# Merging the two halves of the grouped-query mix: two ScalarE copies and a Pool addition, with the queues ordered anew

## The chip, the cores and the metric

One core of one Trainium2 chip. The metric is the device time of one execution in microseconds (us); the time before is the median of three runs. One more execution was taken with the hardware profiler; all rows of the trace are of that one. The engines are TensorE (PE; PEld is its weight load), VectorE (DVE), ScalarE (ACT), Pool (GpSimd) and SyncE (SP), whose queue issues the DMAs.

## What is computed

A one-layer encoder runs over a prompt of 1024 tokens and a sample of 512 tokens, all in float32 with a width of 1024. Cut to what matters here:

```python
h = rmsnorm(x, norm_mix_g)
dq, dk, dv, gq, gk, gv = split(h @ w_in)            # 512, 512, 512, 512, 128, 128 columns
d_out = diff_attention(dq, dk, dv, lam)             # 4 heads, values 128 wide
g_out = gqa_attention(gq, gk, gv)                   # 8 query heads of 64, 2 key/value heads
#   per head: softmax(q k^T * scale) @ v, v is 64 wide
x = x + concat(d_out, g_out) @ w_out
x = x + cross_attention(rmsnorm(x), rmsnorm(mem))
x = x + (silu(a) * b) @ w_down,  [a|b] = dwconv3(rmsnorm(x) @ w_up)
y = rmsnorm(x)
```

The change lies in `softmax(...) @ v` of the grouped-query heads.

## The kernel before

The kernel has two phases with a barrier of all engines between them. The trunk phase makes the input projection and both attentions; the rest phase does the output projection, cross attention and the feed-forward part. The diff touches only the trunk phase, which fills the first 875 us.

The trunk works through six units: four differential heads (units 0 to 3) and two groups of grouped-query heads (units 4 and 5). While one unit's attention runs, TensorE also makes the next unit's projections tile by tile (`proj`, then `nat`, `rope`, `qk_turn`, `qk_hi`, `qk_lo`, `v_split`). During unit 5 no projections are left. A unit's attention goes by pairs: a pair is one head with two query tiles of 128 rows, against 1024 keys (a long pair, prompt) or 512 keys (a short pair, sample). There are 24 differential and 48 grouped-query pairs, 24 in each of units 4 and 5, first the 16 long ones, then the 8 short ones.

The steps of a grouped-query pair are:

- `score` (TensorE, L882 and L883), once per query tile, into one of two PSUM slots `t_scores`
- `max` (VectorE, L1153), `exp` (ScalarE, L1017), `inverse` (VectorE, L1158), `scale` (Pool, L758) on the probabilities in SBUF
- `turn` (TensorE, L896): four transposes of 128x128 for each chunk of 256 keys, into one of two PSUM slots `t_turn`
- `hi` (ScalarE, L1026) and `lo` (VectorE, L1173): the transposed chunk split into a rounded high half and the remainder, each in one of two buffers. The next turn into the same PSUM slot waits for `lo`
- `mix` (TensorE, L917): the chunk's products with the values, summed into the accumulator `t_acc` over all chunks of the pair. The stationary operand holds the values' high half in 64 columns and their low half in the other 64, so rows 0 to 63 of `t_acc` have one part of the result and rows 64 to 127 the other, and both have to be added
- `out` (ScalarE, L1043): copies rows 64 to 127 of `t_acc` into `sq`, after the `merge` of the pair before
- `merge` (VectorE, L1192): adds rows 0 to 63 of `t_acc` and `sq` into `mixed`, after the store of two pairs ago, which read the same slot of `mixed`
- `store` (SyncE, L624): writes `mixed` to DRAM. The first `mix` of the next pair waits for the `merge`, since there is one accumulator

Float32 accuracy of the matmuls comes from such high and low halves, here as everywhere in the kernel.

The order of each engine's queue is not written by hand. `plan` puts each step with a due time, a duration and its predecessors, and `Plan.placed` walks through them: on each engine, the step whose wait goes least beyond that engine's `PATIENCE` comes first, and among those the one with the earliest rank. The rank is the due time moved by a number in `SHIFT`, one for each kind of step and stage (`dl`, `ds`, `gl`, `gs` are long and short pairs of differential and grouped-query units; `g` and `d` are the projections). The result is five fixed queues. The waits in the code stand for the data, so an order changes when a thing runs, not what it computes.

In the same phase Pool also splits the output weights (`out_split`, L681 and L684) during unit 5, and ScalarE and VectorE split the first two tiles of the next phase (`mix_hi` L1048, `mix_lo` L1197). At the end of the phase SyncE issues the last store, all engines meet at the barrier, and TensorE starts with L1981.

Of the kernel before, what the change touches and what calls it, by code (L numbers as in the profile page):

```python
# [33 lines left out]
ALU = mybir.AluOpType  # L34
# [3 lines left out]
P = 128  # L38
# [9 lines left out]
HD = 64  # L48
# [59 lines left out]
def unit_pairs():  # L108
# [4 lines left out]
    for u, (kind, _) in enumerate(UNITS):  # L113
        diff = kind == "diff"
        begin = now
        for seg, (t0, S) in enumerate(SEGS):
# [16 lines left out]

PATIENCE = {"PE": 0.03, "DVE": 0.23, "ACT": 0.36, "POOL": 0.23, "SP": 0.0}
SHIFT = {
    "dl": {"coef": -20.2, "combine": 6, "eps_r": 29.7, "exp": 3.9, "finish": 8.6, "hi": 7.7, "inverse": -50.1, "lo": 9, "max":
          19.8, "mix": 5.2, "out": 11.2, "score": 1.3, "spread": -12.7, "store": 5.4, "sub_mean": 2, "sub_rstd": 11, "sumsq":
          -72.3, "turn": -0.5},
    "ds": {"coef": -18.7, "combine": -16.4, "eps_r": -16.7, "exp": -3.3, "finish": -31.2, "hi": -6.7, "inverse": 43.7, "lo": 8.4,
          "max": -15.7, "mix": 5.1, "out": 7.2, "score": -5.6, "spread": -0.8, "store": 0.8, "sub_mean": 21.1, "sub_rstd": -38.7,  # L140
          "sumsq": -22.8, "turn": 1.8},
    "gl": {"exp": -5.7, "hi": -3.5, "inverse": -0.7, "lo": -21.9, "max": -3.2, "merge": -28.7, "mix": 1, "out": -2.2, "scale": 0.3,
          "score": -1.7, "store": 28.5, "turn": 0.4},
    "gs": {"exp": -4.8, "hi": -4, "inverse": -1.6, "lo": -1.4, "max": -4.5, "merge": -0.6, "mix": -36.7, "out": -2.9, "scale":
          -0.6, "score": -0.2, "store": -13.7, "turn": 2.5},
    "g": {"head_mean": -7.2, "head_norm": -8.8, "head_rstd": 16.7, "nat": -2.6, "proj": 0.1, "qk_hi": -42.5, "qk_lo": 15.5,
         "qk_turn": 0.2, "rope_add": 1.6, "rope": 8, "turn_round": -15.5, "v_split": 16.5},
    "d": {"nat": -42.3, "proj": -2.8, "qk_hi": 47.1, "qk_lo": 19.3, "qk_turn": 0.2, "rope": 5.3, "v_split": 9.7},
}
# [79 lines left out]
def plan(pairs, bounds):  # L229
# [115 lines left out]
    for p in pairs:  # L345
# [40 lines left out]
        whole = ("combine", (p, p.score + 3)) if p.diff else ("scale", (p, p.score + 1))  # L386
        merged = None if prev is None else ("out", (prev,)) if prev.diff else ("merge", (prev,))
        for c in range(p.chunks):
            b = first + space * c
            older = (p, c - 2) if c >= 2 else (prev, prev.chunks + c - 2) if prev else None  # L390
            put("PE", b, 0.46, "turn", (p, c), whole, ("turn", (p, c - 1)) if c else None)
            put("ACT", b + 0.6, 0.6, "hi", (p, c), ("turn", (p, c)), ("mix", older) if older else None)
            put("DVE", b + 1.25, 0.69, "lo", (p, c), ("hi", (p, c)))
            put("PE", b + space + 0.05, 0.72 if p.diff else 0.5, "mix", (p, c), ("lo", (p, c)), ("mix", (p, c - 1)) if c else merged,
                ("v_split", (tiles,)), ("nat", (NT - 1,)) if p.no == 0 else None)
# [10 lines left out]
        else:  # L406
            put("ACT", b, 0.38, "out", (p,), ("mix", (p, p.chunks - 1)), merged)
            put("DVE", b + 0.4, 0.42, "merge", (p,), ("out", (p,)))
            put("SP", b + 1.0, 0.07, "store", (p,), ("merge", (p,)))
# [15 lines left out]
def trunk_phase(nc, sems, a, key_scratch, value_scratch, split_x, mix_scratch, ident, half, wo_hi, wo_lo, wo_raw, h_hi, h_lo, h_raw):  # L425
# [13 lines left out]
    with ExitStack() as ctx:  # L439
# [118 lines left out]
        def stored_before(p):  # L558
            return mixed_stored[p.no % 2], 16 * (p.no // 2)
# [83 lines left out]
        def _(pool):  # L643
            nc.gpsimd.memset(ones[:, :], 1.0).then_inc(consts_made, 1)
            steps = 0
            for _, kind, what in order["POOL"]:
# [107 lines left out]
                elif kind == "scale":  # L754
                    p, n = what
                    pool.wait_ge(inv_done, n - 2 * n_diff + 1)
                    pr = prob[:, n % PSLOTS, 0:p.keys]
                    nc.gpsimd.tensor_scalar(pr, pr, inv[:, n % COLS:n % COLS + 1], 1.0, ALU.mult, ALU.mult).then_inc(scaled, 1)  # L758
                elif kind == "eps_r":
                    p, = what  # L760
# [19 lines left out]
        def _(pe):  # L780
# [7 lines left out]
            for _, kind, what in order["PE"]:  # L788
# [110 lines left out]
                elif kind == "mix":  # L899
# [3 lines left out]
                    if c == 0:  # L903
                        pe.wait_ge(v_split, p.unit * NT + (PT if p.seg == 0 else NT))
                        if p.no > n_diff:
                            pe.wait_ge(merged, p.no - n_diff)
                        elif p.no:
                            pe.wait_ge(copied, p.no)
                        else:
                            pe.wait_ge(nat_filled, NT)  # L910
# [24 lines left out]
        def _(act):  # L935
            for _, kind, what in order["ACT"]:
# [90 lines left out]
                elif kind == "out":  # L1027
# [10 lines left out]
                    else:  # L1038
                        if p.no > n_diff:
                            act.wait_ge(merged, p.no - n_diff)  # L1040
                        else:
                            act.wait_ge(spread_done, n_diff)
                        nc.scalar.copy(sq[0:HD, :], ps_o[HD:P, 0:2 * P]).then_inc(copied, 1)  # L1043
                elif kind == "mix_hi":
# [18 lines left out]
        def _(dve):  # L1063
            steps = 0
            for _, kind, what in order["DVE"]:
# [116 lines left out]
                elif kind == "finish":  # L1182
# [4 lines left out]
                                                   ps_t[:, slot, 0:2 * P], ALU.mult, ALU.mult).then_inc(finished, 1)  # L1187
                elif kind == "merge":
                    p, = what
                    dve.wait_ge(*stored_before(p))  # L1190
                    dve.wait_ge(copied, p.no + 1)
                    nc.vector.tensor_tensor(mixed[0:HD, p.no % 2, :], ps_o[0:HD, 0:2 * P], sq[0:HD, :], ALU.add).then_inc(merged, 1)  # L1192
                elif kind == "mix_lo":
# [1483 lines left out]
```

## Time and profile before

| | before |
|---|---|
| median of 3 runs | 2425.55 us (2425.24 to 2426.47) |
| the profiled execution | 2424.22 us |
| its span in the trace | 2422.4 us |
| TensorE busy | 2358.4 us (97%) |
| VectorE busy | 1695.5 us (70%) |
| ScalarE busy | 1017.0 us (42%) |
| Pool busy | 1393.4 us (58%) |
| mean granted TensorE clock | 0.994 |

The span is what the trace covers; 1.8 us of the profiled execution lie outside it. A row by line names the line of the kernel, the engine, the operation, what it writes and reads with their shapes, the count, the busy time with the mean of one, and how long the engine stood idle just before, with what it then waited for. In a row of a stretch each engine has its busy time with the number of instructions in brackets. TensorE's matmuls overlap in its pipeline, so its busy time is the time in which at least one is in flight.

### The profile page before, as it was taken

Reading aid. Unit: us, or ns where it says so; the run is one execution under the profiler, and the core shown is the slowest. Engines: PE = TensorE matmul, PEld = TensorE weight load, DVE = VectorE, ACT = ScalarE, POOL = GpSimd, SP = SyncE. Lnnn points to the kernel's source line nnn. Section 1 sums busy time; section 2 is a strip of 40 time slices with the busy share of each in tenths; the row PEclk is TensorE's granted clock in tenths of the full one; section 3 lists DMA queues with packets and bytes.
Section 4 is the critical chain, followed back from the end, with each engine's and each line's share of the span. In section 5 each row is a group of like instructions: output and inputs, shape, how many; then the busy total and the mean of one; then the engine's idle time right before and its main releaser. Section 6 shows DMA issues by size and latency. Waiting matters only on the chain.

```text
span 2422.4 us, 34257 instructions
## 1 busy us (share of the span) xinstructions
PE 2358.4 (97%) x12306; PEld 2021.4 (83%) x12306; DVE 1695.5 (70%) x2503; ACT 1017.0 (42%) x2048; POOL 1393.4 (58%) x1603
## 2 busy tenths in 40 slices
PE   7999999999999999999999999999989999999997
PEld 6999888888898878888888888888778888888886
DVE  7537777788989963243334388877688878887887
ACT  4436656555668851133332213211233333333334
POOL 5454645689877630052320277776677777777774
PEclk9999999999999999999999999999999999999999
DMA  8643444432212062131344322322321111111112
GB/s 298 247 174 136 157 144 159 153 129 98 94 61 85 13 195 104 59 116 61 120 144 137 140 95 96 105 95 88 131 98 55 53 53 53 53 53 52 53 53 92
DMA packets 102583, 260.40 MB, mean 107 GB/s; under 512 B 10128, under 2 KB 45328, under 8 KB 91920
## 3 DMA queue, kind: packets, MB, share of 16 engines
q1 hardware_dynamic: 101120, 257.82, 30.9%
q8 instruction: 100, 1.64, 0.3%
q14 instruction: 67, 0.55, 0.1%
q10 hardware_dynamic: 1296, 0.39, 0.1%
HBM read 209.95 MB, written 48.23 MB: 107 GB/s over the span
## 4 chain that ended last, share of the span: by engine, by line
PE 59%; DVE 2%; POOL 1%; issue 1%; ACT 1%; DMA 1%; SPq 0%; POOLq 0%; DVEq 0%; ACTq 0%
PE r_bank L2075 29%; PE r_bank L1981 11%; PE r_bank L1952 10%; PE r_bank L2014 5%; PE r_bank L2033 1%; PE r_bank L2062 1%; PE r_bank L1996 1%; DVE r_conv L2416 1%; PE r_bank L2045 0%; DMA r_rows_w<-in_w_up_units 0%; DVE r_x_p L2575 0%; ACT r_conv L2277 0%; POOL r_s_raw L1861 0%; DVE r_x_p L2564 0%; SPq L1727 0%
## 5 line engine op out<-in xcount | busy, mean ns | idle before, releaser
L843 PE MATMUL t_proj<-t_w_hi,t_hbuf 128*128 128x384 f32 x1056 | 312.7, 349 | 2.1 <-ACT t_nat L994 0.7
L2494 DVE TENSOR_TENSOR r_x_p<-r_bank,r_x_p 128x512 f32<-128x512 f32 x320 | 208.6, 683 | 50.9 <-PE r_bank L2075 50.1
L2416 DVE SCALAR_TENSOR_TENSOR r_conv<-r_rows,r_taps,r_conv 128x511 f32<-128x511 f32 (+1 forms) x132 | 181.8, 1377 | 54.3 <-ACT r_conv L2277 52.0
L1153 DVE TENSOR_REDUCE t_max_neg<-t_scores 128x1 f32<-128x1024 f32 (+1 forms) x192 | 197.0, 1038 | 23.4 <-PE t_scores L877 17.3
L1017 ACT ACTIVATE t_prob<-t_scores,t_max_neg 128x1024 f32<-128x1024 f32 (+1 forms) x192 | 187.3, 977 | 49.9 <-DVE t_max_neg L1153 45.7
L843 PEld LDWEIGHTS t_proj<-t_w_hi,t_hbuf 128*128 128x128 f32 x1056 | 195.7, 190 | 8.3 <-issue 6.8
L1026 ACT CAST t_pt_hi<-t_turn 128x512 fp32r<-128x512 f32 x240 | 140.1, 586 | 108.0 <-PE t_turn L896 82.3
L1173 DVE TENSOR_TENSOR t_pt_lo<-t_turn,t_pt_hi 128x512 fp32r<-128x512 f32 x240 | 163.5, 686 | 29.8 <-ACT t_pt_hi L1026 26.2
L843 PE MATMUL t_proj<-t_w_lo,t_hbuf 128*128 128x384 f32 x528 | 178.5, 338 | 0.0
L1762 POOL TENSOR_TENSOR r_stat<-r_stat,minus_half 128x1 f32<-128x1 f32 x24 | 14.1, 587 | 273.7 <-DVE r_stat L2379 273.7
L1817 POOL TENSOR_TENSOR r_w_lo<-r_stage,r_w_hi 128x1024 fp32r<-128x1024 f32 (+1 forms) x86 | 166.2, 1933 | 7.2
L2246 ACT CAST r_s_hi<-r_s_raw 128x512 fp32r<-128x512 f32 x88 | 54.6, 620 | 229.9 <-POOL r_s_raw L1868 87.0
L896 PE MATMUL t_turn<-ident,t_prob 128*128 128x128 f32 x960 | 142.5, 274 | 6.2 <-DVE t_pt_lo L1173 4.2
L917 PE MATMUL t_acc<-t_pt_hi,t_v_hi 128*128 128x256 f32 x480 | 138.8, 306 | 2.7 <-DVE t_mixed L1192 1.4
L1834 POOL TENSOR_TENSOR r_s_lo<-r_s_raw,r_s_hi 128x512 fp32r<-128x512 f32 x88 | 116.8, 1327 | 39.1 <-ACT r_s_hi L2246 39.1
L1814 POOL TENSOR_SCALAR r_w_hi<-r_stage 128x1024 fp32r<-128x1024 f32 (+1 forms) x86 | 84.4, 982 | 93.6 <-PE r_bank L2075 48.8
L2428 DVE TENSOR_TENSOR r_x_s<-r_bank,r_x_s 128x512 f32<-128x512 f32 x176 | 120.3, 688 | 24.8 <-PE r_bank L2075 23.0
L1952 PE MATMUL r_bank<-r_hs_hi,r_w_hi 128*128 128x512 f32 x352 | 137.1, 389 | 0.0
L1952 PE MATMUL r_bank<-r_hs_lo,r_w_hi 128*128 128x512 f32 x352 | 136.9, 389 | 0.0
L1952 PE MATMUL r_bank<-r_hs_hi,r_w_lo 128*128 128x512 f32 x352 | 136.9, 389 | 0.0
L896 PEld LDWEIGHTS t_turn<-ident,t_prob 128*128 128x128 f32 x960 | 111.8, 140 | 24.5 <-issue 11.8
L2075 PE MATMUL r_bank<-r_wd_lo,r_g_hi 128*128 128x512 f32 x336 | 130.7, 389 | 0.0
(299 smaller groups left out, 7282.3 us busy)
## 6 DMA issues: line engine op xcount, KB each, us to landing
t_hbuf<-split_x SPq DMA_DIRECT2D x60, 1024.0 KB, 4.8
r_stage<-in_w_up_units SPq DMA_DIRECT2D x44, 512.0 KB, 3.2
r_rows_w<-in_w_up_units SPq DMA_DIRECT2D x88, 256.0 KB, 2.9
split_x<-t_hbuf SPq DMA_DIRECT2D x12, 1024.0 KB, 5.2
r_stage<-in_w_down SPq DMA_DIRECT2D x22, 512.0 KB, 3.3
r_wd_raw<-in_w_down SPq DMA_DIRECT2D x42, 256.0 KB, 2.7
t_stage<-in_w_in_units SPq DMA_DIRECT2D x6, 1536.0 KB, 6.6
t_xkv_raw<-in_w_xkv_heads SPq DMA_DIRECT2D x16, 512.0 KB, 5.8
```

The costliest lines, as they stand in the source:

```text
L843: ins = nc.tensor.matmul(proj_bank(i), l, r[:, k, :], start=(k == 0 and j == 0), stop=(k == KT - 1 and j == 2))
L896: ins = nc.tensor.transpose(ps_t[:, slot, kk * 2 * P + qt * P:kk * 2 * P + (qt + 1) * P], prob[:, n % PSLOTS, keys], ident[:, :])
L1017: nc.scalar.activation(prob[:, n % PSLOTS, 0:p.keys], ps_s[:, n % 2, 0:p.keys], ACT.Exp, bias=max_neg[:, n % COLS:n % COLS + 1], accum_out ...
L1026: nc.scalar.copy(pt_hi[:, n % 2, :], ps_t[:, slot, :]).then_inc(pthi_done, 1)
L1153: nc.vector.tensor_reduce(max_neg[:, n % COLS:n % COLS + 1], ps_s[:, n % 2, 0:p.keys], AX.X, ALU.max, negate=True).then_inc(max_done, 1)
L1173: nc.vector.tensor_tensor(pt_lo[:, n % 2, :], ps_t[:, slot, :], f32(pt_hi[:, n % 2, :]), ALU.subtract).then_inc(ptlo_done, 1)
L1817: nc.gpsimd.tensor_tensor(lo, raw, f32(hi), ALU.subtract).then_inc(w_split[s], 1)
L1952: ins = nc.tensor.matmul(one_bank(s), l, r, start=(k == 0 and j == 0), stop=(k == KT - 1 and j == 2))
L1981: ins = nc.tensor.matmul(acc(t)[:, cols], l[:, k, :], r[:, cols], start=(k == 0 and j == 0), stop=(k == KT - 1 and j == 2))
L2075: ins = nc.tensor.matmul(out, l, r, start=(first and j == 0), stop=(last and j == 2), skip_group_check=onto)
L2416: return nc.vector.scalar_tensor_tensor(out, src, tap_of(j, s, i), out, ALU.mult, ALU.add)
L2494: nc.vector.tensor_tensor(x_p[:, t, cols], down_bank(n), x_p[:, t, cols], ALU.add).then_inc(p_add, 1)
```

## The change

`out` of a grouped-query pair now makes two ScalarE copies out of the accumulator: rows 0 to 63 into `mixed` and rows 64 to 127 into `sq`. `merge` moves to Pool and adds `sq` to `mixed` in place in SBUF. The wait for the store of two pairs ago moves with the first writer of `mixed` from VectorE's queue to ScalarE's. The first `mix` of a pair now waits for the copies (`copied`) and not for the merge. In the plan, `out` takes 0.8 in place of 0.38 and `merge` 0.55 on Pool in place of 0.42 on VectorE, with the new predecessors. All of `PATIENCE` but SyncE's and nearly all of `SHIFT` have new values, so that the queues of the whole trunk phase are placed anew.

```diff
-PATIENCE = {"PE": 0.03, "DVE": 0.23, "ACT": 0.36, "POOL": 0.23, "SP": 0.0}
+PATIENCE = {"PE": 0, "DVE": 0.47, "ACT": 0.38, "POOL": 0.72, "SP": 0.0}
 SHIFT = {
...
-    "gl": {"exp": -5.7, "hi": -3.5, "inverse": -0.7, "lo": -21.9, "max": -3.2, "merge": -28.7, "mix": 1, "out": -2.2, "scale": 0.3,
-          "score": -1.7, "store": 28.5, "turn": 0.4},
-    "gs": {"exp": -4.8, "hi": -4, "inverse": -1.6, "lo": -1.4, "max": -4.5, "merge": -0.6, "mix": -36.7, "out": -2.9, "scale":
-          -0.6, "score": -0.2, "store": -13.7, "turn": 2.5},
+    "gl": {"exp": 14.4, "hi": -3.9, "inverse": -2.3, "lo": -13.5, "max": -7.7, "merge": -22.4, "mix": 1.3, "out": -4, "scale":
+          -0.4, "score": -1.5, "store": 26.1, "turn": 0.4},
+    "gs": {"exp": 1.6, "hi": -9.5, "inverse": -1.5, "lo": -1.8, "max": -4, "merge": -44.3, "mix": -23.4, "out": -2.5, "scale": 18,
+          "score": 3.8, "store": -50.6, "turn": 1.1},
...
-            put("ACT", b, 0.38, "out", (p,), ("mix", (p, p.chunks - 1)), merged)
-            put("DVE", b + 0.4, 0.42, "merge", (p,), ("out", (p,)))
+            put("ACT", b, 0.8, "out", (p,), ("mix", (p, p.chunks - 1)), copied if prev.diff else ("merge", (prev,)),
+                ("store", (pairs[p.no - 2],)))
+            put("POOL", b + 0.9, 0.55, "merge", (p,), ("out", (p,)))
...
+                elif kind == "merge":
+                    p, = what
+                    pool.wait_ge(copied, p.no + 1)
+                    nc.gpsimd.tensor_tensor(mixed[0:HD, p.no % 2, :], mixed[0:HD, p.no % 2, :], sq[0:HD, :], ALU.add).then_inc(merged, 1)
...
-                        if p.no > n_diff:
-                            pe.wait_ge(merged, p.no - n_diff)
-                        elif p.no:
+                        if p.no:
                             pe.wait_ge(copied, p.no)
...
+                        act.wait_ge(*stored_before(p))
+                        nc.scalar.copy(mixed[0:HD, p.no % 2, :], ps_o[0:HD, 0:2 * P])
                         nc.scalar.copy(sq[0:HD, :], ps_o[HD:P, 0:2 * P]).then_inc(copied, 1)
...
-                elif kind == "merge":
-                    p, = what
-                    dve.wait_ge(*stored_before(p))
-                    dve.wait_ge(copied, p.no + 1)
-                    nc.vector.tensor_tensor(mixed[0:HD, p.no % 2, :], ps_o[0:HD, 0:2 * P], sq[0:HD, :], ALU.add).then_inc(merged, 1)
```

## Rows read from the trace of the kernel before

**Rows 1.** The page's busy times of the whole span.
```profile
PE 2358.4 (97%) x12306; PEld 2021.4 (83%) x12306; DVE 1695.5 (70%) x2503; ACT 1017.0 (42%) x2048; POOL 1393.4 (58%) x1603
```
**Rows 2.** Stretches (from:to, length): PE, PEld, DVE, ACT, POOL busy, clock, DMA.
```profile
160.00:480.00 320.00, 316.59 (x1965) 282.90 (x1964) 229.24 (x431) 188.20 (x503) 175.79 (x401) 1.00 0.44 155
480.00:597.00 117.00, 112.19 (x691) 97.70 (x690) 100.31 (x186) 67.04 (x154) 102.50 (x179) 1.00 0.34 120
597.00:750.00 153.00, 150.13 (x1018) 140.20 (x1018) 134.98 (x266) 108.59 (x237) 121.06 (x186) 1.00 0.19 65
750.00:830.00 80.00, 78.78 (x563) 71.78 (x562) 77.58 (x134) 71.47 (x132) 63.33 (x62) 1.00 0.22 66
830.00:873.00 43.00, 37.93 (x258) 31.00 (x256) 36.78 (x76) 34.33 (x77) 13.39 (x19) 1.00 0.17 42
...
600.00:620.00 20.00, 18.38 (x126) 16.97 (x126) 16.85 (x32) 12.69 (x27) 18.63 (x29) 1.00 0.26 88
```
**Rows 3.** Waits, 590 to 880: total us, times, longest.
```profile
POOL t_prob L758 <- DVE t_inv L1158: 49.9, 35, 3.9
PE t_turn L896 <- DVE t_pt_lo L1173: 4.2, 5, 1.3
...
PE t_acc L917 <- DVE t_mixed L1192: 1.4, 2, 1.0
PE t_scores L882 <- ACT t_prob L1017: 1.3, 3, 0.7
PE t_acc L917 <- DVE t_pt_lo L1173: 1.2, 2, 0.6
...
PE t_turn L896 <- POOL t_prob L758: 0.9, 1, 0.9
PE t_turn L932 <- DVE t_pt_lo L1173: 0.5, 1, 0.5
```
**Rows 4.** Groups by line on VectorE, 590 to 880.
```profile
L1173 DVE TENSOR_TENSOR t_pt_lo<-t_turn,t_pt_hi 128x512 fp32r<-128x512 f32 x159 | 108.3, 686 | 13.4 <-ACT t_pt_hi L1026 10.9
...
L1192 DVE TENSOR_TENSOR t_mixed<-t_acc,t_sq 64x256 f32<-64x256 f32 x48 | 19.6, 408 | 2.9 <-ACT t_sq L1043 2.0 <-DMA mix_scratch<-t_mixed 0.8
```
**Rows 5.** Groups by line on ScalarE, 750 to 830 (two rows) and 830 to 873.
```profile
L1026 ACT CAST t_pt_hi<-t_turn 128x512 fp32r<-128x512 f32 x55 | 32.3, 587 | 7.9 <-PE t_turn L896 3.7 <-PE t_acc L917 1.0
...
L1043 ACT COPY t_sq<-t_acc 64x256 f32<-64x256 f32 x14 | 5.2, 370 | 0.4
...
L1043 ACT COPY t_sq<-t_acc 64x256 f32<-64x256 f32 x12 | 4.4, 369 | 2.1 <-PE t_acc L917 1.7
```
**Rows 6.** In order of time, the phase's end: start us, length, engine, line.
```profile
870.11 0.37 ACT L1043 COPY t_sq<-t_acc 64x256 f32<-64x256 f32 x1
870.73 0.41 DVE L1192 TENSOR_TENSOR t_mixed<-t_acc,t_sq 64x256 f32<-64x256 f32 x1
871.28 0.36 PE L917 MATMUL t_acc<-t_pt_hi,t_v_hi 128*128 128x256 f32 x1 [0.95 <-DVE t_mixed L1192]
...
872.64 0.37 ACT L1043 COPY t_sq<-t_acc 64x256 f32<-64x256 f32 x1 [1.55 <-PE t_acc L917]
873.11 0.42 DVE L1192 TENSOR_TENSOR t_mixed<-t_acc,t_sq 64x256 f32<-64x256 f32 x1 [1.30 <-ACT t_sq L1043]
...
874.93 0.47 PE L1981 MATMUL r_bank<-wo_hi,h_hi 128*128 128x512 f32 x1 [2.33 <-PEq L439]
```
**Rows 7.** The tile t_mixed: idle before its instructions, and its DMAs' landing.
```profile
  DMA mix_scratch<-t_mixed: 0.8, 1
...
DMA to landing us min/median/max: 1.7/1.9/7.5
```
**Rows 8.** Single lines: nanoseconds min/median/max, first and last start.
```profile
L750 POOL TENSOR_TENSOR t_nat<-t_rot_a,t_rot_b x24: 726/736/764, 483.9 to 747.2; 128x256 f32<-128x256 f32 x24
...
L684 POOL TENSOR_TENSOR wo_lo<-wo_raw,wo_hi x16: 1273/1290/1305, 762.9 to 808.9; 128x512 fp32r<-128x512 f32 x16
...
L1116 DVE TENSOR_TENSOR t_rot_a<-t_nat x24: 472/493/1343, 474.8 to 737.2; 128x320 f32<-128x320 f32 x24
```

More of the change, by code:

```diff
@@ L131 @@
 RING = {"turn": "lo", "qk_turn": "qk_lo", "sumsq": "sub_mean", "spread": "finish", "total": "mean"}
-PATIENCE = {"PE": 0.03, "DVE": 0.23, "ACT": 0.36, "POOL": 0.23, "SP": 0.0}
+PATIENCE = {"PE": 0, "DVE": 0.47, "ACT": 0.38, "POOL": 0.72, "SP": 0.0}
 SHIFT = {
[L136 to L141, printed above, removed]
-    "gl": {"exp": -5.7, "hi": -3.5, "inverse": -0.7, "lo": -21.9, "max": -3.2, "merge": -28.7, "mix": 1, "out": -2.2, "scale": 0.3,
-          "score": -1.7, "store": 28.5, "turn": 0.4},
-    "gs": {"exp": -4.8, "hi": -4, "inverse": -1.6, "lo": -1.4, "max": -4.5, "merge": -0.6, "mix": -36.7, "out": -2.9, "scale":
-          -0.6, "score": -0.2, "store": -13.7, "turn": 2.5},
-    "g": {"head_mean": -7.2, "head_norm": -8.8, "head_rstd": 16.7, "nat": -2.6, "proj": 0.1, "qk_hi": -42.5, "qk_lo": 15.5,
-         "qk_turn": 0.2, "rope_add": 1.6, "rope": 8, "turn_round": -15.5, "v_split": 16.5},
-    "d": {"nat": -42.3, "proj": -2.8, "qk_hi": 47.1, "qk_lo": 19.3, "qk_turn": 0.2, "rope": 5.3, "v_split": 9.7},
@@ new lines @@
+    "dl": {"coef": -7.6, "combine": 21.4, "eps_r": 30, "exp": 5.8, "finish": 15.4, "hi": 10.3, "inverse": -62.4, "lo": 9.9, "max":
+          20.1, "mix": 5.1, "out": 23.7, "score": 1.4, "spread": 1.6, "store": 19.8, "sub_mean": 4.8, "sub_rstd": 22.6, "sumsq":
+          -61.9, "turn": -0.4},
+    "ds": {"coef": 2.9, "combine": -26.7, "eps_r": -30.8, "exp": -2, "finish": -52.6, "hi": -7.8, "inverse": 39.2, "lo": 15.8,
+          "max": -13, "mix": 8.3, "out": -0.2, "score": -8.4, "spread": 5.8, "store": 13.5, "sub_mean": 29, "sub_rstd": -39.7,
+          "sumsq": -50, "turn": 1.5},
@@ new lines @@
+    "gl": {"exp": 14.4, "hi": -3.9, "inverse": -2.3, "lo": -13.5, "max": -7.7, "merge": -22.4, "mix": 1.3, "out": -4, "scale":
+          -0.4, "score": -1.5, "store": 26.1, "turn": 0.4},
+    "gs": {"exp": 1.6, "hi": -9.5, "inverse": -1.5, "lo": -1.8, "max": -4, "merge": -44.3, "mix": -23.4, "out": -2.5, "scale": 18,
+          "score": 3.8, "store": -50.6, "turn": 1.1},
+    "g": {"head_mean": -2.1, "head_norm": 4, "head_rstd": 16.3, "nat": -3.7, "proj": 0.1, "qk_hi": -34.5, "qk_lo": 12.6,
+         "qk_turn": 0.4, "rope_add": -5.4, "rope": 16.2, "turn_round": -18, "v_split": 14.6},
@@ L149 @@
+    "d": {"nat": -27, "proj": -2.6, "qk_hi": 47.7, "qk_lo": 29.7, "rope": 8.4, "v_split": 9.2},
 }
@@ L386, in plan @@
         whole = ("combine", (p, p.score + 3)) if p.diff else ("scale", (p, p.score + 1))
-        merged = None if prev is None else ("out", (prev,)) if prev.diff else ("merge", (prev,))
+        copied = None if prev is None else ("out", (prev,))
         for c in range(p.chunks):
@@ L393, in plan @@
             put("DVE", b + 1.25, 0.69, "lo", (p, c), ("hi", (p, c)))
-            put("PE", b + space + 0.05, 0.72 if p.diff else 0.5, "mix", (p, c), ("lo", (p, c)), ("mix", (p, c - 1)) if c else merged,
+            put("PE", b + space + 0.05, 0.72 if p.diff else 0.5, "mix", (p, c), ("lo", (p, c)), ("mix", (p, c - 1)) if c else copied,
                 ("v_split", (tiles,)), ("nat", (NT - 1,)) if p.no == 0 else None)
```

## The prediction

> **What bounds the kernel now.** I read the busy table first. TensorE is busy 2358.4 us of 2422.4 [rows 1], so all that any edit outside TensorE's own work can give back is 64 us, and most of that is not where the change is. The second view is the table of stretches [rows 2]. It splits the trunk phase by what runs in it: 160 to 480 is the first three differential units, 480 to 597 the last of them beside the first grouped-query projections, 597 to 750 grouped-query unit 4 beside the projections of unit 5, 750 to 830 the long pairs of unit 5, 830 to 873 its short pairs. The reader is to take the stretch less its PE column: 3.4, 4.8, 2.9, 1.2 and 5.1 us, together 17.4 us of idle TensorE. The grouped-query part, where merges run, has 9.2 us of it. The other columns of the same rows tell which helper is closest to full: VectorE has 77.6 of 80 us in the long pairs of unit 5 (97%), ScalarE 71.5 (89%); in the short pairs they have 36.8 and 34.3 of 43; in unit 4 VectorE has 135.0, Pool 121.1 and ScalarE 108.6 of 153. TensorE sits at 98% beside a VectorE at 97%, so a full VectorE doesn't by itself mean a stalled TensorE.
>
> The third view is who TensorE waited for there [rows 3]. Waits for VectorE's low halves (L1173) are 4.2, 1.2 and 0.5 us, together 5.9. Waits for the merge (L1192) are 1.4 us in two places. ScalarE's exponential cost 1.3, Pool's scaling 0.9. The 2.3 us at L439 are the barrier between the two phases. Nothing behind the barrier is touched by the diff, and its order is made by another plan, so the whole argument is about these microseconds and about what the new order does with the 8.2 us ahead of 597.
>
> **What is taken away and what it gives.** 48 additions on VectorE of 408 ns, 19.6 us [rows 4]. They are not on the path by themselves: the two places where TensorE waited for one are worth 1.4 us. The accumulator t_acc is now free when ScalarE's second copy ends. Before, in the next to last pair, ScalarE's copy began at 870.11, the addition began at 870.73 and ended at 871.14, and TensorE went on at 871.28 [rows 6]: 1.03 us from copy to release. Two copies of 0.37 are 0.74, so 0.3 us is gained in each such place and all of the wait only if something else was early too. I take 0.8 us for the two (bounds 0.6 and 1.4).
>
> The larger part is the relief of VectorE's queue: 19.6 us of the 249.8 that it works from 597 to 876, where the low halves wait behind merges. It can give at most the 5.9 us of waits for low halves. I take 2.5, a little under half: VectorE was idle 10.9 us waiting for ScalarE's high half before low halves [rows 4], and that part of their lateness doesn't go when VectorE is emptier. Bounds 0 and 5.9.
>
> **What is added, ScalarE.** One more copy of 64x256 for each of 48 pairs at 369 to 370 ns [rows 5], 17.7 us. The same copy shows 14 times in the long pairs of unit 5 and 12 times in the short ones [rows 5]. In the long pairs ScalarE goes from 71.5 to 71.5 + 14 x 0.37 = 76.7 of 80 us (96%), while VectorE falls by 14 x 0.41 to 71.9: the two change places. In the short pairs it goes from 34.3 to 34.3 + 12 x 0.37 = 38.7 of 43 (90%). A copy out stands ahead of a high half or an exponential in ScalarE's queue, and each such high half comes 0.37 us later. It reaches TensorE where this already waits for low halves: four places in the short pairs, 4 x 0.37 = 1.5 us, which I take. Bounds: nothing, and 24 x 0.37 = 8.9 us if it happens at each pair of unit 5. The cover that hides the rest is TensorE's other queued work (the mix of the chunk before, the scores of the next pair); in unit 5 no projections are left to fill in.
>
> ScalarE now also waits for the store of two pairs ago. Behind it stand the high halves and exponentials of the next pair, and TensorE behind those. A store lands in 1.9 us at the median and 7.5 at most, and VectorE was held up by one once for 0.8 us [rows 7]. That one moves to ScalarE; I count it at nothing (bounds 0 and 0.8), since a pair takes over 3 us and the store is two pairs old.
>
> **What is added, Pool.** 48 additions of 64x256. The trace has none of that shape; the nearest are an addition with 256 columns at 736 ns and, above it, a subtraction with 512 columns at 1290 [rows 8]. From the 256-column row I take 0.74 us; the lower end is half of the first, 0.37, if 64 partitions cost half of 128, the upper 1.29. That is 35.5 us. In unit 4 Pool goes from 121.1 to 121.1 + 24 x 0.74 = 138.8 of 153 us (91%) and becomes the fullest of the three helpers there. A merge ahead of a scaling delays it by 0.74, and the transposes wait for the scaling. Pool stood idle 49.9 us before scalings, waiting for VectorE's reciprocal [rows 3], so nearly all merges fit in those holes; one that doesn't, in the crowded first 20 us of unit 4 [rows 2] or at a late pair, costs 0.7 us. Taken: +0.7. Bounds 0 and 24 x 0.74 = 17.8.
>
> The Trainium skill has a rule against moving this to Pool: "SBUF — State Buffer", section "SBUF: two separate sides", says that VectorE and GpSimd take turns by an exclusive lock on a shared port pair, which a VectorE instruction with two SBUF inputs and a GpSimd instruction that reads SBUF both want. The rows agree that such VectorE work stretches: the square at L1116 has a median of 493 ns and a maximum of 1343 [rows 8]. By the page the removed addition, with one input in PSUM, freed nothing of that lock and the new one takes it.
>
> **The end of the phase.** All engines meet at the barrier. Before, the last copy began at 872.64 and the last merge ended at 873.53, and TensorE's first matmul of the next phase came at 874.93 [rows 6]. The chain is now 0.37 + 0.37 + about 0.1 for the handover (872.64 + 0.37 to 873.11 shows it) + 0.74 on Pool = 1.58 instead of 0.89. Nothing hides it: +0.7 us (bounds 0.3 and 1.2).
>
> **The order placed anew.** Ranks and patience change for all kinds, the differential units too. Nothing in the trace shows the new order. It can give back no more than the 17.4 us of idle [rows 2], less what I counted above, and it can add as much. VectorE's place for low halves is the cause of most waits [rows 3], and it is what ranks decide; with 19.6 us less to place, the plan has more room than before. I take -2.0 us (bounds -9 and +7).
>
> **The sum.** -0.8 - 2.5 + 1.5 + 0 + 0.7 + 0.7 - 2.0 = -2.4 us. The profiled execution took 2424.2 us (span 2422.4 and 1.8 around it), so 2421.8; the median of the runs shown is 1.3 us above it, so 2423.1 us.
>
> **The rivals.** A measurement of this kernel can tell about 0.2%, 4.9 us, from no change: faster means under 2420.7, slower over 2430.4.
> *Most of the idle is given back.* If all 5.9 us of low-half waits and 1.4 us of merge waits go and the new order finds some 2 us more ahead of 597, less 0.7 at the barrier, the sum is -8.6 us: 2417. For it: VectorE is the fullest helper in each grouped-query stretch. Against it: ScalarE is put at 96% in its place, and much of the low halves' lateness comes from ScalarE.
> *ScalarE takes VectorE's place as what is late* (the slower side). In the long pairs of unit 5 it has 3 us of slack in 80 after the change. If its second copy delays a high half in each of the 24 pairs and TensorE has nothing else queued, 24 x 0.37 = 8.9 us, with 0.7 at the barrier and little given back: +8.5, 2434. It decides from the point where TensorE runs out of ready mixes, as it does already in the short pairs. Against it: from 750 to 830 ScalarE was idle 7.9 us ahead of high halves, of which the row names 4.7 as waits for TensorE [rows 5].
> *Pool is late in unit 4.* 91% full, with every scaling on the path to the transposes: half of 24 merges that each push a scaling by 0.74 are 8.9 us: 2433. For it: Pool was already 18.6 of 20 us busy from 600 to 620, where TensorE stood idle 1.6 us [rows 2], over half of what it lost in unit 4; a lock that stretches both sides would add to it. By the skill's page each clash could hold either engine for a whole instruction.
> *It does nothing that can be seen*: TensorE's work is the same and the waits only change their names: 2425.
>
> **How the numbers follow.** The forecast's case has 0.52; its own range is 2417 to 2429, and about a third of it (0.18) lies under 2420.7, so it gives 0.18 to faster and 0.34 to same. The idle given back has 0.18 (faster), nothing to be seen 0.06 (same), ScalarE late 0.14 and Pool late 0.10 (slower). Together faster 0.36, same 0.40, slower 0.24. The range leaves out the far part of the best and the worst cases: 2414.5 to 2433.5.
>
> **What the profile after would show.** Right: L1192 gone from VectorE, 96 copies of 0.37 us on ScalarE, waits of TensorE for L1173 down to about 3 us between 597 and 873, no wait for a merge, Pool's addition near 0.74 us, and 0.7 us more between the last copy and the first L1981. Wrong: waits of L896 or L917 for low halves that stand or grow, with VectorE idle before them for L1026 (ScalarE's rival); L896 waiting for L758 in several places (Pool's); or the idle from 160 to 597 moving by more than 2 us, which would say that the order and not the merge decided.

## The result and the profile after

| | before | after |
|---|---|---|
| median | 2425.49 us | 2442.23 us (2441.49 to 2442.81, 4 runs) |
| span of the profiled execution | 2422.4 us | 2440.1 us |
| ratio | | 1.0069, 95% interval 1.0055 to 1.0085 |

The change makes the kernel 16.7 us slower. I had forecast 2423.1 us within 2414.5 to 2433.5.

The page's busy times after the change, as [rows 1] has them before:

```profile
PE 2366.4 (97%) x12306; PEld 2024.2 (83%) x12306; DVE 1690.9 (69%) x2455; ACT 1030.8 (42%) x2096; POOL 1422.5 (58%) x1651
```

TensorE runs the same 12306 matmuls and is 8.0 us longer busy, where the span grew by 17.7. So nearly half of the loss isn't idle time in this view. The clock doesn't explain it: from the 25th grouped-query copy to the 48th TensorE is 4.3 us longer busy (107.4 against 103.1) for 725 and 728 matmuls, at a granted clock of 1.00 in both. That its busy time takes in short gaps between overlapped matmuls is my reading; no row shows the gaps. I had taken the span less the busy time [rows 1] as all there is to move.

The loss is complete when the next phase starts. L1981 began at 874.93 [rows 6] and begins now at 892.48:

```profile
889.54 0.37 ACT L1047 COPY t_mixed<-t_acc 64x256 f32<-64x256 f32 x1 [1.55 <-PE t_acc L920]
889.92 0.37 ACT L1048 COPY t_sq<-t_acc 64x256 f32<-64x256 f32 x1
...
890.37 0.71 POOL L763 TENSOR_TENSOR t_mixed<-t_mixed,t_sq 64x256 f32<-64x256 f32 x1 [2.18 <-ACT t_sq L1048]
...
892.48 0.47 PE L1981 MATMUL r_bank<-wo_hi,h_hi 128*128 128x512 f32 x1 [2.98 <-PEq L440]
```

Who waited for whom from 590 to 900, after (in all us, times, longest us), against [rows 3] and [rows 4]:

```profile
ACT t_pt_hi L1029 <- PE t_turn L901: 38.4, 54, 3.5
DVE t_pt_lo L1178 <- ACT t_pt_hi L1029: 30.6, 63, 2.5
POOL t_mixed L763 <- ACT t_sq L1048: 25.5, 25, 2.7
POOL t_prob L759 <- DVE t_inv L1163: 21.5, 21, 3.4
PEld t_acc L920 <- DVE t_pt_lo L1178: 17.4, 35, 1.8
...
PE t_acc L920 <- DVE t_pt_lo L1178: 7.2, 12, 1.3
```

The last two lines are the ones to see. TensorE waited 1.2 us for low halves at its mixes before [rows 3] and now waits 7.2; its weight loads waited 5.4 us and now wait 17.4. The second line looks as strong, and isn't. VectorE waited 10.9 us for high halves before low halves and now waits 30.6, but in e13_old_short_both, a run below that loses only 2.5 us, it waits 24.9:

```profile
DVE t_pt_lo L1180 <- ACT t_pt_hi L1031: 24.9, 52, 2.1
```

In e8 and e10, which lose 12 us with a merge's work still on VectorE, it waits 11.4 and 10.6. This wait says that VectorE's queue has become emptier, and not how much is lost. Pool's own free time before scalings fell from 49.9 to 21.5 us, and it stands 25.5 us waiting for copies.

Two stretches of 170 us, each from 1.9 us behind the end of the first grouped-query copy: 597 to 767 before and 602.7 to 772.7 after (columns as in [rows 2]):

```profile
597.00:767.00 170.00, 166.37 (x1128) 154.17 (x1128) 151.55 (x297) 124.21 (x266) 131.32 (x196) 1.00 0.22 73
```
```profile
602.70:772.70 170.00, 162.62 (x1077) 149.27 (x1076) 145.96 (x261) 125.13 (x280) 140.18 (x213) 0.99 0.20 66
```

VectorE and TensorE both do less in the same time (51 matmuls fewer), Pool and ScalarE, which got the work, do more. The most loaded helper, VectorE, went from 89% to 86%, so it isn't that a new engine is full: Pool is at 82%. But VectorE was relieved of 48 additions, 19.6 us in all, and over the whole span its busy time fell by only 4.6 us (1695.5 to 1690.9). Other work of it takes longer. The timeline of Pool and VectorE in the changed kernel shows such a case:

```profile
641.96 0.73 POOL L763 TENSOR_TENSOR t_mixed<-t_mixed,t_sq 64x256 f32<-64x256 f32 x1 [0.74 <-ACT t_sq L1048]
642.12 2.81 DVE L1127 TENSOR_SCALAR t_vstat<-t_vstat 128x5 f32<-128x5 f32 x1
642.68 2.22 POOL L759 TENSOR_SCALAR t_prob<-t_prob,t_inv 128x1024 f32<-128x1024 f32 x2
```

L1127 takes 0.173 us at the median. Here it began beside Pool's new addition and ended when that addition and two scalings right behind it were done, 2.81 us later.

To see where the 17 us arise I read, from the timeline of ScalarE, when the copy into `sq` ended for the 1st, the 25th and the 48th grouped-query pair: in before 595.1, 764.4 and 873.0 us. The first marks the end of the differential units, the second the first pair of unit 5. For each kernel the table gives what was lost against before ahead of the first, between the first two (unit 4) and between the last two (unit 5), all in us from one profiled execution each. "Loss" is the median less the median of before beside which it was timed; with 4 to 10 runs each (one run of e7 at 3360 us, with a granted clock of 0.65, is left out), an interval of up to about 0.15% on either side (3.6 us) belongs to it, so differences of 1 or 2 us between rows are not told apart by it alone.

| kernel | queues | ScalarE's new copy | the addition | loss | ahead | unit 4 | unit 5 |
|---|---|---|---|---|---|---|---|
| changed kernel | new | whole | Pool | 16.7 | 5.7 | 5.8 | 5.8 |
| e5_short_copy | new | 1 column | Pool | 14.1 | 4.7 | 4.6 | 3.9 |
| e6_short_merge | new | whole | Pool, 1 column | 8.1 | 5.5 | -2.5 | 4.6 |
| e7_short_both | new | 1 column | Pool, 1 column | 4.7 | 5.4 | -1.7 | 1.4 |
| e11_spread_earlier | new, one step moved | whole | Pool | 16.7 | 5.0 | 5.3 | 5.8 |
| e4_old_code_new_queues | new | none | VectorE | 24.0 | 5.7 | 6.9 | 9.5 |
| e3_old_queues | old | whole | Pool | 15.7 | -0.3 | 6.5 | 8.3 |
| e14_old_short_copy | old | 1 column | Pool | 11.7 | 1.2 | 4.8 | 5.4 |
| e12_old_short_merge | old | whole | Pool, 1 column | 8.8 | 0.9 | 2.8 | 4.4 |
| e13_old_short_both | old | 1 column | Pool, 1 column | 2.5 | 0.2 | 0.7 | 1.2 |
| e8_dve_adds | old | whole | VectorE, in SBUF | 12.1 | 0.5 | 3.6 | 8.3 |
| e9_later_merges | old, merges later | whole | Pool | 17.9 | -0.4 | 6.9 | 10.8 |
| e10_pool_only | old | none (VectorE copies) | Pool | 11.8 | -0.2 | 5.8 | 5.0 |
| e15_new_code_replanned | searched | whole | Pool | 16.4 | 5.9 | 5.0 | 6.0 |
| e16_old_code_replanned | searched | none | VectorE | 11.2 | 7.4 | -2.0 | 7.3 |

### The profile page after: what moved, and what is told of

Its sections match the earlier page's. It is cut to its first block, busy times and chain, and to the rows that moved or that the text cites. A ratio compares the mean times of both kernels' runs of the same rounds, so it can differ in the third digit from the quotient of the medians.

```text
span 2440.1 us, 34257 instructions
## 1 busy us (share of the span) xinstructions
PE 2366.4 (97%) x12306; PEld 2024.2 (83%) x12306; DVE 1690.9 (69%) x2455; ACT 1030.8 (42%) x2096; POOL 1422.5 (58%) x1651
## 4 chain that ended last, share of the span: by engine, by line
PE 58%; DVE 2%; POOL 1%; issue 1%; ACT 1%; DMA 1%; SPq 0%; POOLq 0%; DVEq 0%; ACTq 0%
PE r_bank L2075 29%; PE r_bank L1981 11%; PE r_bank L1952 10%; PE r_bank L2014 5%; PE r_bank L2033 1%; PE r_bank L2062 1%; PE r_bank L1996 1%; DVE r_conv L2416 1%; PE r_bank L2045 0%; DMA r_rows_w<-in_w_up_units 0%; DVE r_x_p L2575 0%; ACT r_conv L2277 0%; POOL r_s_raw L1861 0%; DVE r_x_p L2564 0%; SPq L1727 0%
## 5 line engine op out<-in xcount | busy, mean ns | idle before, releaser
L1762 POOL TENSOR_TENSOR r_stat<-r_stat,minus_half 128x1 f32<-128x1 f32 x24 | 14.1, 589 | 266.4 <-DVE r_stat L2379 266.4
L920 PE MATMUL t_acc<-t_pt_hi,t_v_hi 128*128 128x256 f32 x480 | 141.7, 310 | 9.3 <-DVE t_pt_lo L1178 7.4
L901 PE MATMUL t_turn<-ident,t_prob 128*128 128x128 f32 x960 | 142.2, 275 | 8.0 <-DVE t_pt_lo L1178 3.2
L2075 PE MATMUL r_bank<-r_wd_hi,r_g_hi 128*128 128x512 f32 x336 | 130.7, 389 | 0.0
```

The source lines that it names most:

```text
L901: ins = nc.tensor.transpose(ps_t[:, slot, kk * 2 * P + qt * P:kk * 2 * P + (qt + 1) * P], prob[:, n % PSLOTS, keys], ident[:, :])
L920: ins = nc.tensor.matmul(ps_o[:, 0:2 * P], l, r, start=(c == 0 and kk == 0 and j == 0), stop=(c == p.chunks - 1 and kk == 1 and j == len(t ...
L2075: ins = nc.tensor.matmul(out, l, r, start=(first and j == 0), stop=(last and j == 2), skip_group_check=onto)
```

## The experiments

### Code and order crossed

Theory O said that the new order is what costs, theory S that the added work does. The first run makes the plan of before with its own values and its own model, and then only carries the merges over; the second is the opposite cross.

```diff
+    merges = [z for z in order["DVE"] if z[1] == "merge"]
+    order["DVE"] = [z for z in order["DVE"] if z[1] != "merge"]
+    order["POOL"] = sorted(order["POOL"] + merges, key=lambda z: z[0])
```

> The changed code (two ScalarE copies, Pool's addition) in the queues of the kernel before: its plan is made with the old values and the old model, then each merge is taken out of VectorE's queue and put into Pool's at its planned time; nothing else moves. Theory O (the new order is what costs): 2423 to 2428 us, since the code alone moves few waits. Theory S (the added copy on ScalarE and the merge on Pool cost it, whatever the order): 2436 to 2446 us.

Measured: 2440.1 us, a loss of 15.7. The new code alone, in the old order, costs all that the change costs. Theory O falls. The order placed anew has given back nothing in sum that these runs can tell. It has moved the loss: none ahead of the first copy in e3 and 5.7 us in the changed kernel, but 8.3 us in unit 5 in e3 and 5.8 there.

> The opposite cross: the code of before (one ScalarE copy, VectorE's merge out of the accumulator) in the queues of the changed kernel, each merge taken from Pool's queue to VectorE's at its planned time. Theory O: 2438 to 2446 us, nearly all of the loss is there without the new code. Theory S: 2424 to 2432 us.

Measured: 2448.4 us, a loss of 24.0, above what either theory had and on the side of theory O. Here VectorE's merges stand where Pool's were planned, and TensorE waits for them:

```profile
PE t_acc L921 <- DVE t_mixed L1196: 14.8, 20, 1.8
```

So the new queues are bad for the old code, while the old queues serve the new code as well as its own do (15.7 against 16.7). These two runs alone don't say which part of the new code is dear.

### The added work cut, in both sets of queues

The added copy or Pool's addition is cut to one column. The instruction, its waits and its place stay. The expectations speak of two theories. In theory P, Pool's addition is what delays; in theory A, ScalarE's second copy is.

```diff
-                        nc.scalar.copy(mixed[0:HD, p.no % 2, :], ps_o[0:HD, 0:2 * P])
+                        nc.scalar.copy(mixed[0:HD, p.no % 2, 0:1], ps_o[0:HD, 0:1])
```
```diff
-                    nc.gpsimd.tensor_tensor(mixed[0:HD, p.no % 2, :], mixed[0:HD, p.no % 2, :], sq[0:HD, :], ALU.add)...
+                    nc.gpsimd.tensor_tensor(mixed[0:HD, p.no % 2, 0:1], mixed[0:HD, p.no % 2, 0:1], sq[0:HD, 0:1], ALU.add)...
```

> The changed kernel with the added ScalarE copy cut to one column, so that rows 0 to 63 of the grouped-query mix are mostly not copied; queues and waits unchanged. Theory S, ScalarE's part: 2430 to 2435 us, 8 to 12 us come back. Theory O: 2438 to 2442 us, at most 4 come back.

Measured: 2438.5 us, a loss of 14.1: 2.6 us came back. That is in theory O's range and not in that of theory S, so I had ScalarE's part too large here.

> The changed kernel with Pool's addition cut to one column, so that the grouped-query result is mostly not added up; queues and waits unchanged. Theory S, Pool's part: 2432 to 2437 us, 5 to 10 us come back. Theory O: 2439 to 2442 us; about 0.6 us come back at the barrier in any case.

Measured: 2432.5 us, a loss of 8.1: 8.6 us came back, 0.5 of them at the barrier (2.40 us from the last copies to L1981 in place of 2.94). That is in theory S's range for Pool's part.

> The changed kernel with both the added ScalarE copy and Pool's addition cut to one column (rows 0 to 63 mostly not copied, the halves mostly not added up), queues and waits as in the changed kernel. If the loads of both engines add up to the loss: 2424 to 2428 us. If a part of the loss comes from the order itself (who stands behind whom), it stays: 2429 to 2434 us.

Measured: 2429.9 us, a loss of 4.7 (interval 1.0009 to 1.0028), in the range of the case in which a part stays with the order.

> The changed code in the queues of before with ScalarE's added copy cut to one column (rows 0 to 63 mostly not copied); Pool makes its whole addition. Theory P for unit 4 and A for unit 5: 2431 to 2435 us, with 3 to 4 us lost in the first eight pairs of unit 4 as in the run e10_pool_only, and under 4 in unit 5. If Pool alone makes the loss everywhere: 2436 to 2440 us.

Measured: 2436.5 us, a loss of 11.7, above the range for Pool in unit 4 and ScalarE in unit 5, and in the range of Pool alone. In unit 5 the loss is 5.4, not under 4: Pool costs there too.

> The changed code in the queues of before (e3_old_queues, 2440.1 us) with Pool's addition cut to one column, so that the halves are mostly not added up. VectorE is relieved of the merge, Pool hardly loaded, only ScalarE has its second copy. Theory A (the second copy lies on a chain through the engines in unit 5 with its full 0.37 us for each of 24 pairs): 2433 to 2437 us, with 7 to 9 us lost in unit 5. If VectorE's relief outweighs the copy: 2424 to 2429 us.

Measured: 2433.6 us, a loss of 8.8, but only 4.4 of it in unit 5, where theory A had 7 to 9: the number was met and the place wasn't.

> The changed code in the queues of before with both the added copy and the addition cut to one column (rows 0 to 63 mostly not copied, halves mostly not added). In the changed kernel's queues the same cuts gave 2429.9 us. If what is left there is the order's own loss: 2423 to 2426 us here. If it is the fixed cost of two more instructions and a longer hand-over for each pair: 2428 to 2431 us.

Measured: 2427.3 us, a loss of 2.5 (interval 1.0001 to 1.0019), between the two cases.

Groups by line from 590 to 890 show what was cut. First e14_old_short_copy, then e12_old_short_merge:

```profile
L765 POOL TENSOR_TENSOR t_mixed<-t_mixed,t_sq 64x256 f32<-64x256 f32 x48 | 35.1, 731 | 12.9 <-ACT t_sq L1050 12.9
...
L1049 ACT COPY t_mixed<-t_acc 64x1 f32<-64x1 f32 x48 | 7.3, 152 | 13.1 <-PE t_acc L922 7.1 <-POOL t_mixed L765 4.1 <-DMA mix_scratch<-t_mixed 1.5
```
```profile
L765 POOL TENSOR_TENSOR t_mixed<-t_mixed,t_sq 64x1 f32<-64x1 f32 x48 | 8.9, 185 | 20.1 <-ACT t_sq L1050 20.1
...
L1049 ACT COPY t_mixed<-t_acc 64x256 f32<-64x256 f32 x48 | 17.5, 365 | 8.0 <-PE t_acc L922 6.9 <-DMA mix_scratch<-t_mixed 0.5
```

The cut addition runs 26.2 us less on Pool (48 x 0.546). That was worth 8.6 us in the new queues (9.4 beside a short copy) and 6.9 us in the old ones (9.2 beside a short copy). The cut copy runs 10.2 us less on ScalarE and was worth 2.6 (3.4) and 4.0 (6.3) us. So what was cut of the addition weighs more in every pairing. For each us cut the copy is at least as dear (0.25 to 0.62 us against 0.26 to 0.36), and less than two thirds of it was cut, so the whole copy can cost as much as the whole addition. Both values are larger when the other part is small, which would mean that they share what they delay, but by 0.8 and 2.3 us only, within the noise. Pool still stands 20.1 us waiting for copies in e12, more than in e3 (17.4), and e12 loses 6.9 us less. So what costs is that the addition runs its 0.73 us, and not that a merge blocks the queue while it waits.

How does it cost? In unit 4 the traces point at what it does to VectorE. Three VectorE steps of the projections work in SBUF alone (the square into `t_rot_a`, the scaling in place of `t_vstat` and the multiplication into `t_nat`). Between the 1st and the 25th copy, with the same number of instructions on both sides, they take 3.6 us more in e3 than in e12, 3.7 more in e14 than in e13, 8.2 more in the changed kernel than in e6 and 8.8 more in e5 than in e7. The loss in unit 4 grows in these pairings by 3.7, 4.1, 8.3 and 6.3 us. TensorE's waits put down to Pool's scalings are 0.9 us in e13 and in e14 alike. So these four pairings agree that in unit 4 the price comes mostly by way of VectorE and not by way of late scalings. No run has the addition without this effect, so it isn't tested by itself. In unit 5 VectorE has no such steps, and the addition costs 3.9 and 4.2 us in the old queues and 1.2 and 2.5 in the new ones; in e14 ScalarE's copy waits there 3.8 us for Pool's merge of the pair before, in the changed kernel no such wait shows. What the rest of unit 5's price is stays open.

Pool's holes were not where I had needed them. Of its 49.9 us of waits before scalings [rows 3] the kernel before has 1.8 from 590 to 665, the first pairs of unit 4:

```profile
POOL t_prob L758 <- DVE t_inv L1158: 1.8, 2, 1.6
```

From 665 to 764.4 it has 17.2, and in unit 5 30.9. In e14, from 595 to 665, it is the same: Pool's idle time is made of waits of single projection steps for VectorE, and almost none stands ahead of a scaling:

```profile
L761 POOL TENSOR_SCALAR t_prob<-t_prob,t_inv 128x1024 f32<-128x1024 f32 x19 | 22.0, 1163 | 1.0 <-DVE t_inv L1165 1.0
...
L734 POOL TENSOR_TENSOR t_nat<-t_nat,t_head_gain 128x320 f32<-128x320 f32 x6 | 5.2, 870 | 3.6 <-DVE t_nat L1135 3.6
...
L765 POOL TENSOR_TENSOR t_mixed<-t_mixed,t_sq 64x256 f32<-64x256 f32 x7 | 5.1, 733 | 0.0
```

Seven merges put 5.1 us into a Pool that waited 1.0 us before its scalings, and the first eight pairs took 3.3 us longer than before (copy 1 to copy 8; 4.6 by copy 8 less the 1.2 ahead of copy 1), against 0.7 in e13.

### Each engine's part by itself

> In the queues of the kernel before, exactly: ScalarE makes both copies, VectorE adds the two halves in SBUF at the merge's old place, Pool does nothing new. Theory P (Pool's merge is what delays, through the scalings behind it): 2426 to 2430 us, only the second copy costs. Theory A (ScalarE's second copy delays the high halves): 2434 to 2440 us.

ScalarE copies both halves and VectorE adds them in SBUF in the merge's old place; Pool has nothing new. Measured: 2437.4 us, a loss of 12.1, in theory A's range, 8.3 us of it in unit 5 (8.9 had been the price of the rival). But VectorE's addition isn't the one of before. With both inputs in SBUF it takes 29.9 us for 48 in place of 19.6, and 7.1 us of the difference lie in unit 5. The worst stand beside Pool's splitting of the output weights, each more than three times its median of 0.418 us:

```profile
786.88 1.33 DVE L1191 TENSOR_TENSOR t_mixed<-t_mixed,t_sq 64x256 f32<-64x256 f32 x1
793.16 1.34 DVE L1191 TENSOR_TENSOR t_mixed<-t_mixed,t_sq 64x256 f32<-64x256 f32 x1
```

So the 8.3 us aren't the copy's price alone. e12, where VectorE is relieved and Pool has a short addition, loses 8.8. The 3.3 us between them hold this stretching, so they don't say what the relief of VectorE is worth, and the two intervals overlap.

> In the queues of before: ScalarE makes its one copy, VectorE copies rows 0 to 63 out of the accumulator at the merge's old place (about the merge's duration), Pool adds. ScalarE and VectorE have the load they had. Theory P: 2434 to 2439 us. Theory A: 2425 to 2429 us.

Here `merge` in VectorE's queue becomes a copy of rows 0 to 63 (406 ns, as the merge was) and Pool adds. Measured: 2437.0 us, a loss of 11.8: theory P. With ScalarE and VectorE loaded as before, this is the cost of Pool's addition with a longer hand-over: ScalarE waits 6.7 us for Pool's merges, and the steps into `t_rot_a` and `t_nat` take 5.1 us more in unit 4 than before. Both e8 and e10 lose about 12 us, both parts together 15.7 (e3). The two can't be added, since in e3 VectorE has no merge and in e8 and e10 it has one.

> The changed code in the queues of before (as in the run e3_old_queues, 2440.1 us), each merge put into Pool's queue 1.5 us later in planned time, so that it stands behind scalings that would otherwise wait behind a merge that waits for its copies. Theory P by blocking: 2431 to 2436 us. Theory P by load alone, or theory A: 2438 to 2442 us.

```diff
-    order["POOL"] = sorted(order["POOL"] + merges, key=lambda z: z[0])
+    order["POOL"] = sorted(order["POOL"] + [(z[0] + 1.5, *z[1:]) for z in merges], key=lambda z: z[0])
```

Measured: 2443.2 us, a loss of 17.9, no better than e3's 15.7. Pool's waits for copies fell from 17.4 to 10.2 us, and nothing was gained; ScalarE's copy now waited 5.7 us for Pool's merge of the pair before (2.8 in e3). So it isn't a clean test: the delay took one wait away and made another. It gives blocking no support.

### One wait that the plan doesn't know

The changed kernel loses 5.7 us ahead of its first grouped-query copy. In its timeline ScalarE stands 3.84 us in front of that copy, and TensorE then waits 2.31 us; behind that idle time the granted clock is 0.83 over the 10 us from 600, which I work out as some 3.4 us at the lower of its two levels (1.2 GHz), and two projections in a row take 0.79 us in place of 0.51. ScalarE, then TensorE, of the changed kernel:

```profile
600.06 0.37 ACT L1047 COPY t_mixed<-t_acc 64x256 f32<-64x256 f32 x1 [3.84 <-issue]
```
```profile
602.29 0.63 PE L901 MATMUL t_turn<-ident,t_prob 128*128 128x128 f32 x4 [2.31 <-DVE t_pt_lo L1178]
...
603.10 0.79 PE L848 MATMUL t_proj<-t_w_hi,t_hbuf 128*128 128x384 f32 x2
```

The code waits there for the spread of the last differential pair, and the plan has no such predecessor in either kernel. In the old queues the spread came at 590.98, long before; in the new ones at 599.39, behind projections. e11 moves it ahead of them.

```diff
+    pe = order["PE"]
+    late = max(n for n, z in enumerate(pe) if z[1] == "spread")
+    pe.insert(late - 2, pe.pop(late))
```

> The changed kernel with one step moved: TensorE's spread of the last differential pair goes ahead of the two projection steps that it stood behind. ScalarE's first grouped-query copy waits for it (3.8 us in the changed kernel's trace), with high halves and exponentials behind it. Theory W (this one wait starts the first 5.7 us of the loss): 2437 to 2440 us, and the first grouped-query copy ends near 598 us instead of 600.8. Theory L (the loss is spread over the load of the helpers, and the early 5.7 us only shift work): 2441 to 2443 us.

Measured: 2441.5 us, against 2424.8 beside it, a loss of 16.7, in theory L's range. The first copy ends at 600.1, not near 598. The edit didn't take the wait away: the spread now waits 1.24 us for its PSUM slot, and ScalarE still stands 3.22 us.

```profile
598.62 0.67 PE L939 MATMUL t_turn<-t_sq,t_ones 128*128 128x256 f32 x2 [1.24 <-DVE t_qk L1157]
...
599.38 0.37 ACT L1051 COPY t_mixed<-t_acc 64x256 f32<-64x256 f32 x1 [3.22 <-issue]
```

So theory W wasn't tested by it. What e6 and e7 show is that the lead lost ahead of the first copy is partly work moved: with a light Pool they win 2.5 and 1.7 us back in unit 4. With both loads cut the loss is 4.7 us in the new order and 2.5 in the old one, and the two intervals overlap.

### Placed for the real durations

The plan gives Pool's addition 0.55 us; the trace has 0.73. The last two runs ask if that is the fault.

```diff
-            put("POOL", b + 0.9, 0.55, "merge", (p,), ("out", (p,)))
+            put("POOL", b + 0.9, 0.76, "merge", (p,), ("out", (p,)))
...
-            ... copied if prev.diff else ("merge", (prev,)),
+            ... ("spread", (prev,)) if prev.diff else ("merge", (prev,)),
```

> The changed code with queues placed for what the trace shows: in the plan Pool's addition takes 0.76 in place of 0.55 (0.73 us measured), the first grouped-query copy out has the last spread as predecessor, and PATIENCE and SHIFT are searched anew from the changed kernel's values with that plan (13 minutes, keep what shortens the planned trunk). Theory O2 (the loss is mostly an order placed for a Pool that is faster than the real one): 2424 to 2431 us. Theory P (Pool's added 35 us cost 7 to 9 us in whatever order): 2432 to 2440 us.

> The code of before, with the last spread as predecessor of the first grouped-query copy in the plan and PATIENCE and SHIFT searched anew for the same time as in e15. It tells how much a search alone gives. If before's order was near its best: 2422 to 2427 us. If the search is worth as much as it is for the changed code: under 2420 us.

Measured: 2441.8 and 2436.7 us, losses of 16.4 and 11.2. The first is above both ranges. The control (e16, the code of before) missed its range by 10 us: in its own plan TensorE's last step of the trunk begins 2.8 us earlier than before (855.4 against 858.2), and on the chip the kernel is 11.2 us slower. The plan isn't close enough for differences of this size. Yet it had a warning: in the plan of the changed kernel, as its code has it, that step begins at 865.7, 7.5 us later than before. So e15 can't say what the best order for the new code would give; under the same method the new code stands 5 us behind the old. Whether an order exists that wins back Pool's price stays open. No version found here beats the kernel before.

## Why the prediction was wrong

**The barrier: right.** From the start of the last copies to L1981 it was 2.29 us [rows 6] and is 2.94; 0.65 more, where I had 0.7.

**The accumulator: right in kind.** No merge holds TensorE any more; three waits for the copy remain, 1.3 us in all, against 1.4 before. Of the 0.8 us hardly anything is left. The wait for the store, taken at nothing, cost nothing: no wait of ScalarE for one shows in the changed kernel.

**VectorE's relief: it didn't arrive.** I had 2.5 us for 19.6 us less to do. In the changed kernel VectorE's busy time fell by only 4.6 us; with Pool's addition cut to a column (e6) it fell by 14.0. No run measures what the relief alone gives; with both added loads cut to a column (e13) the kernel is still 2.5 us slower than before. The waits of TensorE for low halves, which were to fall from 5.9 to about 3, rose: L920 alone has 7.2, and its weight loads 17.4 against 5.4 before. I had named waits of VectorE for L1026 that grow as the sign of ScalarE's rival. They grew to 30.6 us, but they do so wherever VectorE is relieved, in e13 too, so the sign tells nothing.

**ScalarE's copy: under-sized.** Taken at 1.5 us. Cutting less than two thirds of its time gave 2.6 to 6.3 us. I had counted the four places where TensorE already waited; the copy makes new ones. The rival put 8.9 us in unit 5. With VectorE relieved and Pool's addition short (e12) the loss there is 4.4 us, with the stretched additions of e8 8.3; the rival's full price isn't shown. I had given it 0.14.

**Pool's addition: the step that failed.** Its duration was right (0.74 taken, 0.731 measured, median), and unit 4's first pairs were the place named. The price was 0.7 us and is 7 to 9 us for the three quarters of it that were cut. The reason given for it, that 49.9 us of waits before scalings are holes for 35 us of merges, fails twice. It added up holes over two units and didn't ask when they lie: 1.8 us of them are in the first pairs of unit 4. And a late scaling was the only path that had a price. The stretching of VectorE was named, with the rows' 1343 ns, and stood in the sum at nothing; in unit 4 it is 3.6 to 8.8 us of VectorE's time, beside 3.7 to 8.3 us of loss. The sign of Pool's rival, transposes (L896, now L901) that wait for scalings in several places, hardly showed: 1.7 us in 3 places, 0.9 in one before.

Unit 5 shows that free time isn't cover. Here are 80 us, mostly of its long pairs, in e13_old_short_both and in e14_old_short_copy, which differ by the addition only, the second taken 5.1 us later since e14 is that much behind at the 25th copy (columns as in [rows 2]):

```profile
750.00:830.00 80.00, 78.06 (x557) 71.07 (x556) 72.03 (x117) 71.45 (x146) 64.68 (x77) 1.00 0.23 67
```
```profile
755.10:835.10 80.00, 75.65 (x522) 66.97 (x521) 67.93 (x112) 67.50 (x137) 71.34 (x76) 1.00 0.22 66
```

Pool is 6.7 us busier, and all others got less done in the same 80 us. TensorE made 35 matmuls fewer, which at 80/557 us each are 5.0 us of work, of which its idle time shows 2.4. Pool had 15.3 us free in the first row, and yet a third of what it was given came through over the whole trunk (9.2 of 26.2 us).

**The order: overrated.** Taken at -2.0, bounds -9 and +7. Between e3 and the changed kernel it did about nothing in sum (15.7 and 16.7 us); with the loads cut it costs some 2, which is within the noise. My sign for an order that decides was idle time of TensorE from 160 to 597 that moves by more than 2 us; it went from 8.2 to 9.9.

**Why the range missed.** The two rivals on the slower side were taken as alternatives of 8.9 us each. (For Pool's, 8.9 us on 2425.5 are 2434 and not the 2433 that I wrote.) Both parts cost at once, and the upper end of the range, 2433.5, had room for one. That two prices near 9 us came close to the sum of what happened is partly luck: Pool's came by another path and was half in unit 5 in the old queues, and ScalarE's isn't shown in full. The rule on the shared port of SBUF, which "SBUF — State Buffer" of the Trainium skill gives in "SBUF: two separate sides", was no small matter, and the traces agree with it. VectorE's SBUF addition in e8 has a median of 0.418 us and runs over 1 us 7 times, at most 1.54, where the merge out of PSUM never took more than 0.417. The other side shows it less: Pool's addition in the changed kernel has a median of 731 ns and a maximum of 990.

```profile
L1191 DVE TENSOR_TENSOR t_mixed<-t_mixed,t_sq x48: 405/418/1544, 596.8 to 885.4; 64x256 f32<-64x256 f32 x48
```
```profile
L763 POOL TENSOR_TENSOR t_mixed<-t_mixed,t_sq x48: 715/731/990, 600.9 to 890.4; 64x256 f32<-64x256 f32 x48
```

## What to carry to other kernels

Where TensorE is 97% busy and fed by a ring of three engines in fixed order, moving work off the fullest helper gains at most what its queue delayed and costs what it delays elsewhere, here a quarter to over a third of every microsecond added on Pool, an engine with 20% free. Look also at what the moved work does to the engine that it leaves: here VectorE was relieved of 19.6 us of additions and its busy time fell by 4.6. Free time of an engine is cover only where it stands ahead of the step that is late; look for it in the stretch, before that step, and not in a sum over the stage. After such a change, time the code in the old order first, and don't book a gain for the new one.

## What had not been expected

TensorE's busy time for the same 12306 matmuls rose by 8.0 us, so busy time holds nearly half of the loss in this kernel. A VectorE step on 5 columns, 0.173 us at the median, took 2.81 us beside Pool's addition and scalings. A planned order that its own model calls shorter was 11.2 us slower on the chip for unchanged code (e16). Pool's two-input addition takes the same time on 64 partitions as on 128: 731 ns for 64x256 against 736 for 128x256 [rows 8].
